# Four split tiles in place of two for the out-projection's activations, converted one weight slot ahead

## The chip, the cores and the metric

The kernel runs on one core of one Trainium2 chip. The metric is the device time of one execution in microseconds (us), taken as the median of several runs.

## What is computed

The reference is a two-layer backbone. Each layer has three parts, each a residual update of the token stream: a SwiGLU FFN, a mixer (a Fourier half and an mLSTM half with four heads), and a second FFN. 512 latent and 256 context tokens are 6 tiles of 128 rows, 1024 channels wide, all in float32. What matters here is the last step of every part, a product with an output weight, and the normalized, gated add behind it:

```python
def swiglu(h, w_in_ff, w_out_ff):
    gu = h @ w_in_ff
    g, u = gu[..., :D_FF], gu[..., D_FF:]
    return (jax.nn.silu(g) * u) @ w_out_ff          # D_FF = 2816

def _ffn_sublayer(x, mod, j, nw_pre, nw_post, w_in_ff, w_out_ff):
    shift, scale, gate = _mod(mod, j)
    y = swiglu(_pre(x, nw_pre, shift, scale), w_in_ff, w_out_ff)
    return x + FFN_RES * gate * rmsnorm(y, nw_post)
...
    return jnp.concatenate([yf, ym], axis=-1) @ w_out   # the mixer's last step
```

## The kernel before

**Split operands.** Every large product runs as three TensorE products of rounded operands: hi·hi, hi·lo and lo·hi, where hi is the operand copied to the engine's reduced float32 form and lo is what the copy lost. ScalarE (ACT) makes each hi with a copy, VectorE (DVE) each lo with a subtraction.

**Weight slots.** Weights come in slots of 128 x 2048 values (1 MB). There is one landing buffer `raw` and there are two pairs `w_hi`, `w_lo`. SyncE (SP) issues the load of slot n once `w_lo` of slot n - 1 is done (L981 for the out-projection). ACT makes `w_hi` (L1021) when the load has landed and TensorE has used slot n - 2. DVE makes `w_lo` behind it (L1183). Only the end of `w_lo` frees `raw`, so loading, `w_hi` and `w_lo` of successive slots follow each other in a ring.

**The out-projection.** A part has two token groups (g = 0, 1) of three tiles each; the last part has one group of four tiles, and the mixer of layer 1 has three tiles and then one. A group runs through `k_slots` weight slots: 11 in an FFN, 4 in a mixer. A slot has two halves (c = 0, 1), each one 128-row chunk of the contraction. `project_out` (L1428) waits for the slot's `w_lo`, then for each half waits for that half's `hj_lo`, and issues 18 matmuls of 128x512 (3 tiles, 3 products, 2 output halves). It raises the semaphore `w_used` after each half.

**The split activations.** `hj` (ACT L1023, DVE L1186) splits one 128x384 chunk of the hidden activations into `hj_hi[b]` and `hj_lo[b]`, b = 0 or 1. Half hs uses tile hs mod 2, and its conversion waits until half hs - 2 has been used:

```python
act.wait_ge(S["w_used"], hs - 1 + START)
```

The engines' queues are in order. In a slot s both ACT and DVE do: `hj` of the slot's own second half, then the weight split of slot n + 1, then `hj` of the next slot's first half. In the mixer's first group the first two are done earlier (`first_out`).

**What else stands in these queues.** In the first group of the first slots DVE reads two gate rows (`gate_half`, L1231) that TensorE has made after the slot. In both FFNs of layer 0 the first eight slots of the first group also hold a *modulation unit* each (L1197 and L1209, fed by loads of `w_ada`); after every fourth, TensorE sums its result (`finish_col`, L1452) before it goes on. Between the groups `evacuate` copies the three output tiles out of PSUM on DVE (L1293), and ACT takes their mean squares (L1067). In the second group the first slots carry *stages* of the first group's normalization behind their conversions: the gated product on DVE (L1268), the residual add on GpSimd (L1006), statistics on ACT (L1051), and transposes on TensorE (L1481).

Of the kernel before, what the change touches and what calls it, by code (L numbers as in the profile page):

```python
# [28 lines left out]
P = 128  # L29
# [9 lines left out]
GW = 384  # L39
# [121 lines left out]
def build(nc, x_in, w_ada, norm_w, w_ff_in, w_ff_out, w_in, w_gates, w_out, w_qkv, cvec_in, gate_b_in,  # L161
          b_col_in, nw_col_in, convw_in, convb_in, hn_w_in, fmix_in, dft_l_in, dft_c_in, dft_g_in, tri_in, out):
    ctx = ExitStack()
    with ctx:  # L164
# [7 lines left out]
        xn_lo = inner.enter_context(nc.sbuf_tensor("xn_lo", [P, KC, TOK], F32R))  # L172
        inner.close()
        arena = sb("arena", [P, XN + 2 * HG])
        hj_hi = [sb(f"hj_hi{i}", [P, GW], F32R) for i in range(2)]
        hj_lo = [sb(f"hj_lo{i}", [P, GW], F32R) for i in range(2)]
        raw = sb("raw", [P, SLOT])
        w_hi = [sb(f"w_hi{i}", [P, SLOT], F32R) for i in range(2)]
        w_lo = [sb(f"w_lo{i}", [P, SLOT], F32R) for i in range(2)]
# [830 lines left out]
        def _(act):  # L1010
# [12 lines left out]
            def hj(sub, g, c, hs, b):  # L1023
                if g == 0:

                    if sub["kind"] == "ffn":
                        act.wait_ge(S["h_done"], c + (sub["proj"] + 1))
                    elif c < HEADS:
                        act.wait_ge(S["f_sb"], HEADS * sub["mix"] + c + 1)
                    else:  # L1030
                        act.wait_ge(S["mix_done"], HEADS * sub["mix"] + c - HEADS + 1)

                act.wait_ge(S["w_used"], hs - 1 + START)
                w = sub["groups"][g] * P
                nc.scalar.activation(split_h(sub, b)[0][:, 0:w], hidden(sub, g, c), ACT.Copy).then_inc(S["hj_hi"], 1)  # L1035

# [62 lines left out]
            def first_out(sub):  # L1099

                nb = sub["slot"] + sub["in_slots"]
                for c in range(2):
                    hj(sub, 0, c, 2 * nb + c, c)

            for t in range(NT):
                act.dma_start(x[:, t, :], x_in[t]).then_inc(S["x_in"], 16)
# [14 lines left out]
            for sub in SUBS:  # L1121
# [18 lines left out]
                for g in range(len(sub["groups"])):  # L1140
                    nb = n0 + sub["in_slots"] + g * sub["k_slots"]
                    pb = nb % 2
                    early = sub["kind"] == "mix" and g == 0
                    if not early:
                        hj(sub, g, 0, 2 * nb, 0)
                    if g == 1:
                        evacuate(sub, 0)
                    done = 0
                    for s, n, par, half, u, st in out_steps(sub, g, loop, 0):
                        if not (early and s == 0):  # L1150
                            hj(sub, g, s * 2 + 1, n * 2 + 1, 1)
                        split_w(n + 1, (pb + par + 1) % 2)
                        if not (isinstance(s, int) and s == sub["k_slots"] - 1):
                            hj(sub, g, s * 2 + 2, n * 2 + 2, 0)
                        if st is not None:
                            stage(sub, 0, st)
                            done = st + 1
# [13 lines left out]
        def _(dve):  # L1171
# [14 lines left out]
            def hj(sub, g, c, q, hs, b):  # L1186
                w = sub["groups"][g] * P
                hi, lo = split_h(sub, b)
                dve.wait_ge(S["hj_hi"], q + 1)
                dve.wait_ge(S["w_used"], hs - 1 + START)  # L1190
                nc.vector.tensor_tensor(lo[:, 0:w], hidden(sub, g, c), hi[:, 0:w].bitcast(F32), ALU.subtract).then_inc(S["hj_lo"], 1)  # L1191

            def unit(count, u):
# [103 lines left out]
            def first_out(sub):  # L1297

                nb = sub["slot"] + sub["in_slots"]
                for c in range(2):  # L1300
                    hj(sub, 0, c, sub["hj"] + c, 2 * nb + c, c)


            dve.wait_ge(S["consts"], 16 * 8)
# [23 lines left out]
            for sub in SUBS:  # L1328
# [29 lines left out]
                for g in range(len(sub["groups"])):  # L1358
                    nb = n0 + sub["in_slots"] + g * sub["k_slots"]
                    q0 = sub["hj"] + g * 2 * sub["k_slots"]  # L1360
                    pb = nb % 2
                    early = sub["kind"] == "mix" and g == 0
                    if not early:
                        hj(sub, g, 0, q0, 2 * nb, 0)
                    if g == 1:
                        evacuate(sub, 0)
                    done = 0
                    for s, n, par, half, u, st in out_steps(sub, g, own.loop, 0):
                        if not (early and s == 0):
                            hj(sub, g, s * 2 + 1, s * 2 + (q0 + 1), n * 2 + 1, 1)  # L1370
                        split_w(n + 1, (pb + par + 1) % 2)
                        if not (isinstance(s, int) and s == sub["k_slots"] - 1):
                            hj(sub, g, s * 2 + 2, s * 2 + (q0 + 2), n * 2 + 2, 0)
                        if not sub["final"] and g == 0 and isinstance(s, int) and s < 2:
                            gate_half(sub, s, 6)
                        if half is not None:
                            unit(4 * half[2] - 16 + u, u)
                            if u == 3:
                                finish_col(half[2], half[1], 6)
                        if st is not None:  # L1380
                            stage(sub, 0, st)
                            done = st + 1
# [15 lines left out]
        def _(pe):  # L1398
# [28 lines left out]

            def project_out(sub, g, s, n, par, q0, first, last):  # L1428

                halves = [split_h(sub, c) for c in range(2)]  # L1430
                hi = w_hi[par][:].rearrange("p (c n) -> p c n", c=2)
                lo = w_lo[par][:].rearrange("p (c n) -> p c n", c=2)
                pe.wait_ge(S["w_lo"], n + 1 + START)
# [204 lines left out]
```

## Time and profile before

| What | Value |
|---|---|
| Median of 3 runs | 3081.69 us (3077.54 to 3083.17) |
| Span of the profiled execution | 3078.4 us |
| TensorE busy | 2796.1 us (91%) |
| DVE busy | 1455.6 us (47%) |
| ACT busy | 839.5 us (27%) |
| GpSimd busy | 84.6 us (3%) |
| Mean granted TensorE clock | 0.958 of full |

The span is from the first to the last instruction of one execution; it is the only time of that execution in the profile. Matmuls overlap in the trace, so a busy TensorE may still be short of its pace; the waits and the start times tell more than the busy share. The eleven stretches in which `project_out` runs take 101 to 111 us per FFN group of three tiles, 36 to 42 us per mixer group, and 121 us for the last part.

### The profile page before, as it was taken

What the parts mean: (1) busy time and instruction counts of PE and PEld (TensorE: products, weight loads), DVE (VectorE), ACT (ScalarE), POOL (GpSimd) and SP (SyncE); (2) the same over time, 40 slices, a digit from 0 to 9 for tenths busy, and PEclk for the clock granted to TensorE, in tenths of its full rate; (3) what the DMA queues carried; (4) which work ended last, traced back from release to release, by engine and by line L of the source; (5) the groups of instructions that cost most, each with busy time, mean ns of one, the idle gap of its engine ahead of it and who ended that gap; (6) DMA issues with size and microseconds to landing.
All of it is one profiled execution on the core that took longest, in us unless ns stands there. A gap on an engine that the chain in (4) does not pass through costs nothing. (4 is left out here: it accounts for less than half of the span.)

```text
span 3078.4 us, 35860 instructions
## 1 busy us (share of the span) xinstructions
PE 2796.1 (91%) x14352; PEld 2474.5 (80%) x14352; DVE 1455.6 (47%) x1975; ACT 839.5 (27%) x1128; POOL 84.6 (3%) x40
## 2 busy tenths in 40 slices
PE   5999999898988869999999899999997978599997
PEld 2999997777865769999877799998777756388876
DVE  2454546455444455455554545542355555532232
ACT  3211112443322431111224311112343522422222
POOL 0000000000000010000000100000001000100001
PEclk9999999998988989999999999999998999799999
DMA  5233344332200213333332233422332300222222
GB/s 208 83 117 129 109 136 127 106 110 73 76 1 1 96 69 115 131 109 132 120 131 96 96 123 109 136 84 81 109 105 91 103 1 28 82 97 98 100 87 82
DMA packets 98664, 298.95 MB, mean 97 GB/s; under 512 B 6672, under 2 KB 23056, under 8 KB 87056
## 3 DMA queue, kind: packets, MB, share of 16 engines
q1 hardware_dynamic: 91440, 280.42, 26.7%
q10 hardware_dynamic: 7136, 17.30, 1.6%
q8 instruction: 62, 1.02, 0.1%
q14 instruction: 26, 0.21, 0.0%
HBM read 295.60 MB, written 2.10 MB: 97 GB/s over the span
## 5 line engine op out<-in xcount | busy, mean ns | idle before, releaser
L1423 PE MATMUL ps<-xn_hi,w_hi 128*128 128x384 f32 (+2 forms) x2496 | 705.9, 345 | 33.2 <-DVE xn_lo L1261 19.6
L1423 PE MATMUL ps<-xn_lo,w_hi 128*128 128x384 f32 (+2 forms) x2496 | 701.6, 343 | 0.0
L1423 PE MATMUL ps<-xn_hi,w_lo 128*128 128x384 f32 (+2 forms) x2496 | 701.4, 343 | 0.0
L1183 DVE TENSOR_TENSOR w_lo<-raw,w_hi 128x2048 fp32r<-128x2048 f32 x195 | 444.8, 2281 | 358.9 <-ACT w_hi L1021 356.1
L1423 PEld LDWEIGHTS ps<-xn_hi,w_hi 128*128 128x128 f32 x2496 | 459.1, 190 | 48.0 <-DVE xn_lo L1261 20.8
L1423 PEld LDWEIGHTS ps<-xn_lo,w_hi 128*128 128x128 f32 x2496 | 460.0, 190 | 12.3
L1423 PEld LDWEIGHTS ps<-xn_hi,w_lo 128*128 128x128 f32 x2496 | 459.7, 190 | 12.5
L1021 ACT ACTIVATE w_hi<-raw 128x2048 fp32r<-128x2048 f32 x195 | 369.7, 1896 | 216.2 <-DMA raw<-w_ff_out 87.5
L1442 PE MATMUL ps<-w_hi,hj_hi 128*128 128x512 f32 x952 | 312.4, 410 | 78.6 <-DVE hj_lo L1191 65.8
L1209 DVE SCALAR_TENSOR_TENSOR acc<-raw_ada,silu_c,acc 128x512 f32<-128x512 f32 x512 | 345.5, 746 | 4.6 <-DVE acc L1197 3.2
L1442 PE MATMUL ps<-w_lo,hj_hi 128*128 128x512 f32 x952 | 303.8, 401 | 0.0
L1442 PE MATMUL ps<-w_hi,hj_lo 128*128 128x512 f32 x952 | 303.0, 400 | 0.0
L1136 ACT ACTIVATE arena<-ps 128x384 f32 (+1 forms) x132 | 57.6, 489 | 883.0 <-PE ps L1423 883.0
L1442 PEld LDWEIGHTS ps<-w_hi,hj_hi 128*128 128x128 f32 x952 | 177.8, 194 | 136.2 <-DVE hj_lo L1191 64.7
L1442 PEld LDWEIGHTS ps<-w_lo,hj_hi 128*128 128x128 f32 x952 | 185.2, 195 | 41.0
L1442 PEld LDWEIGHTS ps<-w_hi,hj_lo 128*128 128x128 f32 x952 | 184.9, 194 | 40.8
L1352 DVE TENSOR_TENSOR arena<-arena,ps 128x384 f32 (+1 forms) x132 | 67.3, 551 | 286.9 <-ACT arena L1136 284.9
L1006 POOL TENSOR_TENSOR x<-x,arena 128x1024 f32<-128x1024 f32 x32 | 83.9, 2625 | 2989.9 <-DVE arena L1268 2989.9
L1191 DVE TENSOR_TENSOR hj_lo<-arena,hj_hi 128x384 fp32r<-128x384 f32 (+1 forms) x164 | 87.9, 541 | 151.6 <-ACT hj_hi L1035 135.2
L1035 ACT ACTIVATE hj_hi<-arena 128x384 fp32r<-128x384 f32 (+2 forms) x164 | 82.3, 505 | 214.4 <-PE ps L1442 214.3
L760 PE MATMUL ps<-xn_hi,w_hi 128*128 128x384 f32 (+1 forms) x320 | 105.0, 368 | 13.3 <-DVE xn_lo L1261 9.8
L1222 DVE TENSOR_TENSOR vecs<-ps,b_col 128x8 f32 (+1 forms) x36 | 6.0, 166 | 209.5 <-PE ps L1452 208.0
(190 smaller groups left out, 2388.3 us busy)
## 6 DMA issues: line engine op xcount, KB each, us to landing
raw<-w_ff_in SPq DMA_DIRECT2D x88, 1024.0 KB, 5.4
raw<-w_ff_out SPq DMA_DIRECT2D x77, 1024.0 KB, 4.9
raw_ada<-w_ada SPq DMA_DIRECT2D x128, 512.0 KB, 3.8
raw<-w_out SPq DMA_DIRECT2D x16, 1024.0 KB, 4.8
raw<-w_in SPq DMA_DIRECT2D x12, 1024.0 KB, 5.3
arena<-w_ada SPq DMA_DIRECT2D x4, 2048.0 KB, 17.4
gate_row<-norm_w ACTq DMA_DIRECT2D x12, 512.0 KB, 4.3
arena<-dft_l_in ACTq DMA_DIRECT2D x2, 2048.0 KB, 8.1
```

The source lines that it names most:

```text
L760: ins = mm(ps[:, ch % 3 + 3 * g, 0:wd], w[:, k, c * P:(c + 1) * P], xx[:, k, g * GW:g * GW + wd], start=(k == 0 and i == 0), stop=(k == KC ...
L1006: nc.gpsimd.tensor_tensor(x[:, t, :], x[:, t, :], ys(i), ALU.add).then_inc(S["x_new"], 1)
L1021: nc.scalar.activation(w_hi[par][:, 0:width], raw[:, 0:width], ACT.Copy).then_inc(S["w_hi"], 1)
L1035: nc.scalar.activation(split_h(sub, b)[0][:, 0:w], hidden(sub, g, c), ACT.Copy).then_inc(S["hj_hi"], 1)
L1136: ins = nc.scalar.activation(dst, ps[:, s * 4 + 2 * g, 0:w], ACT.Silu)
L1183: nc.vector.tensor_tensor(w_lo[par][:, 0:width], raw[:, 0:width], w_hi[par][:, 0:width].bitcast(F32), ALU.subtract).then_inc(S["w_lo"], 1)
L1191: nc.vector.tensor_tensor(lo[:, 0:w], hidden(sub, g, c), hi[:, 0:w].bitcast(F32), ALU.subtract).then_inc(S["hj_lo"], 1)
L1209: ins = nc.vector.scalar_tensor_tensor(out=acc[:, s, :], in0=raw_ada[u % 2][:, c, :], scalar=silu_c[:, k, s:s + 1], in1=acc[:, s, :], op0= ...
L1222: nc.vector.tensor_tensor(dst, ps[:, bank_, GW:GW + 8].rearrange("p (c s) -> p c s", s=2), bias, ALU.add).then_inc(S["fin_read"], 1)
L1352: ins = nc.vector.tensor_tensor(hd, hd, ps[:, s * 4 + 2 * g + 1, 0:w], ALU.mult)
L1423: ins = mm(ps[:, 4 * b + 2 * g + c, col:col + wd], w[:, k, c, :], xx[:, k, t0:t0 + wd], start=(k == 0 and i == 0), stop=(k == KC - 1 and i ...
L1442: ins = mm(ps[:, 2 * i + hf, :], xx[:, i * P:(i + 1) * P], w[:, c, hf * 512:(hf + 1) * 512], start=first and c == 0 and a == 0, stop=last ...
```

## The change

`hj_hi` and `hj_lo` get four tiles each. Slot parity `par` uses tiles 2·par and 2·par + 1, so a conversion waits for half hs - 4 to have been used. Both conversions of a slot are moved into the slot before it: the first half's ahead of that slot's weight split, the second half's behind it. A group's first two conversions both stand at its start, ahead of `evacuate`. In the last part the tiles are slices of `xn_hi` and `xn_lo`, as before, now four of them. The scratch that the compiler keeps for dynamic DMA is set to 4096 bytes.

```diff
-        hj_hi = [sb(f"hj_hi{i}", [P, GW], F32R) for i in range(2)]
-        hj_lo = [sb(f"hj_lo{i}", [P, GW], F32R) for i in range(2)]
+        hj_hi = [sb(f"hj_hi{i}", [P, GW], F32R) for i in range(4)]
+        hj_lo = [sb(f"hj_lo{i}", [P, GW], F32R) for i in range(4)]
...
-                act.wait_ge(S["w_used"], hs - 1 + START)
+                act.wait_ge(S["w_used"], hs - 3 + START)
...
                     if not early:
-                        hj(sub, g, 0, 2 * nb, 0)
+                        for c in range(2):
+                            hj(sub, g, c, 2 * nb + c, 2 * pb + c)
                     if g == 1:
                         evacuate(sub, 0)
                     done = 0
                     for s, n, par, half, u, st in out_steps(sub, g, loop, 0):
-                        if not (early and s == 0):
-                            hj(sub, g, s * 2 + 1, n * 2 + 1, 1)
-                        split_w(n + 1, (pb + par + 1) % 2)
-                        if not (isinstance(s, int) and s == sub["k_slots"] - 1):
-                            hj(sub, g, s * 2 + 2, n * 2 + 2, 0)
+                        more = not (isinstance(s, int) and s == sub["k_slots"] - 1)
+                        ahead = (pb + par + 1) % 2
+                        if more:
+                            hj(sub, g, s * 2 + 2, n * 2 + 2, 2 * ahead)
+                        split_w(n + 1, ahead)
+                        if more:
+                            hj(sub, g, s * 2 + 3, n * 2 + 3, 2 * ahead + 1)
...
-                halves = [split_h(sub, c) for c in range(2)]
+                halves = [split_h(sub, 2 * par + c) for c in range(2)]
...
-    nc = bacc.Bacc("TRN2", target_bir_lowering=False, num_devices=1)
+    nc = bacc.Bacc("TRN2", target_bir_lowering=False, num_devices=1, dynamic_dma_scratch_size=4096)
```

DVE's queue is changed in the same way as ACT's, which is shown.

## Rows read from the trace of the kernel before

**Rows 1.** The page's head.
```profile
span 3078.4 us, 35860 instructions
```

**Rows 2.** Waits of the whole run: us in total, times, longest us.
```profile
PE ps L1442 <- DVE hj_lo L1191: 65.8, 48, 4.1
```

**Rows 3.** Timeline, layer 1, first FFN, first group: start, length, instruction [idle <-releaser].
```profile
2213.93 2.29 DVE L1183 TENSOR_TENSOR w_lo<-raw,w_hi 128x2048 fp32r<-128x2048 f32 x1 [6.18 <-ACT w_hi L1021]
...
2216.83 0.70 PE L1442 MATMUL ps<-w_hi,hj_hi 128*128 128x512 f32 x2 [1.01 <-DVE hj_lo L1191]
...
2221.06 1.92 ACT L1021 ACTIVATE w_hi<-raw 128x2048 fp32r<-128x2048 f32 x1 [4.62 <-DMA raw<-w_ff_out]
...
2223.01 2.29 DVE L1183 TENSOR_TENSOR w_lo<-raw,w_hi 128x2048 fp32r<-128x2048 f32 x1 [5.86 <-ACT w_hi L1021]
2225.22 0.55 DVE L1191 TENSOR_TENSOR hj_lo<-arena,hj_hi 128x384 fp32r<-128x384 f32 x1
2225.69 1.22 DVE L1293 COPY arena<-ps 128x1024 f32<-128x1024 f32 x1
```

**Rows 4.** Timeline, layer 0, mixer, second group: one slot of its stage loop.
```profile
1046.93 2.29 DVE L1183 TENSOR_TENSOR w_lo<-raw,w_hi 128x2048 fp32r<-128x2048 f32 x1 [1.19 <-ACT w_hi L1021]
...
1049.80 1.28 DVE L1268 SCALAR_TENSOR_TENSOR arena<-arena,stat,gate_row 128x1024 f32<-128x1024 f32 x1
1051.16 2.39 POOL L1006 TENSOR_TENSOR x<-x,arena 128x1024 f32<-128x1024 f32 x1 [349.81 <-DVE arena L1268]
...
1055.39 1.90 ACT L1021 ACTIVATE w_hi<-raw 128x2048 fp32r<-128x2048 f32 x1
...
1056.13 0.73 PE L1442 MATMUL ps<-w_hi,hj_hi 128*128 128x512 f32 x2 [1.83 <-DVE hj_lo L1191]
```

**Rows 5.** Timeline, layer 0, first FFN, first group: stretch with modulation units.
```profile
481.92 2.74 DVE L1209 SCALAR_TENSOR_TENSOR acc<-raw_ada,silu_c,acc 128x512 f32<-128x512 f32 x4
...
485.18 0.73 PE L1442 MATMUL ps<-w_hi,hj_hi 128*128 128x512 f32 x2 [1.58 <-DVE hj_lo L1191]
...
492.22 1.92 ACT L1021 ACTIVATE w_hi<-raw 128x2048 fp32r<-128x2048 f32 x1 [2.05 <-DMA raw<-w_ff_out]
...
495.70 2.28 DVE L1183 TENSOR_TENSOR w_lo<-raw,w_hi 128x2048 fp32r<-128x2048 f32 x1
...
510.64 1.92 PE L1452 MATMUL ps<-ones,acc 128*128 128x1 f32 x16 [2.28 <-DVE acc L1209]
...
522.58 0.53 ACT L1035 ACTIVATE hj_hi<-arena 128x384 fp32r<-128x384 f32 x1 [3.57 <-PE ps L1442]
523.01 1.90 ACT L1021 ACTIVATE w_hi<-raw 128x2048 fp32r<-128x2048 f32 x1
```

**Rows 6.** Timeline, the copies between that FFN's two groups.
```profile
576.92 3.49 DVE L1293 COPY arena<-ps 128x1024 f32<-128x1024 f32 x3 [1.85 <-PE ps L1442]
```

**Rows 7.** Timeline, mixers: layer 0 first slot, weights, copies, last slot; layer 1 copies.
```profile
1009.08 2.29 DVE L1183 TENSOR_TENSOR w_lo<-raw,w_hi 128x2048 fp32r<-128x2048 f32 x1
...
1016.23 1.92 ACT L1021 ACTIVATE w_hi<-raw 128x2048 fp32r<-128x2048 f32 x1 [8.56 <-DMA raw<-w_out]
...
1039.22 3.48 DVE L1293 COPY arena<-ps 128x1024 f32<-128x1024 f32 x3
...
1076.29 1.90 ACT L1021 ACTIVATE w_hi<-raw 128x2048 fp32r<-128x2048 f32 x1
...
2626.39 0.28 DVE L1191 TENSOR_TENSOR hj_lo<-arena,hj_hi 128x128 fp32r<-128x128 f32 x1
2626.59 2.35 DVE L1293 COPY arena<-ps 128x1024 f32<-128x1024 f32 x2
```

**Rows 8.** Timeline, TensorE after a wait, second group of layer 0's first FFN.
```profile
584.79 1.21 PE L1442 MATMUL ps<-w_hi,hj_hi 128*128 128x512 f32 x2 [2.17 <-DVE hj_lo L1191]
...
586.66 1.05 PE L1442 MATMUL ps<-w_hi,hj_lo 128*128 128x512 f32 x2
...
588.32 0.62 PE L1442 MATMUL ps<-w_lo,hj_hi 128*128 128x512 f32 x2
```

More of the change, by code:

```diff
@@ L1102, in first_out @@
                 for c in range(2):
-                    hj(sub, 0, c, 2 * nb + c, c)
+                    hj(sub, 0, c, 2 * nb + c, nb % 2 * 2 + c)
             for t in range(NT):
@@ L1189, in hj @@
                 dve.wait_ge(S["hj_hi"], q + 1)
-                dve.wait_ge(S["w_used"], hs - 1 + START)
+                dve.wait_ge(S["w_used"], hs - 3 + START)
                 nc.vector.tensor_tensor(lo[:, 0:w], hidden(sub, g, c), hi[:, 0:w].bitcast(F32), ALU.subtract).then_inc(S["hj_lo"], 1)
@@ L1300, in first_out @@
                 for c in range(2):
-                    hj(sub, 0, c, sub["hj"] + c, 2 * nb + c, c)
+                    hj(sub, 0, c, sub["hj"] + c, 2 * nb + c, nb % 2 * 2 + c)
             dve.wait_ge(S["consts"], 16 * 8)
@@ L1363, in _ @@
                     if not early:
-                        hj(sub, g, 0, q0, 2 * nb, 0)
+                        for c in range(2):
+                            hj(sub, g, c, q0 + c, 2 * nb + c, 2 * pb + c)
                     if g == 1:
@@ L1368, in _ @@
                     for s, n, par, half, u, st in out_steps(sub, g, own.loop, 0):
[L1369 to L1373, printed above, removed]
+                        more = not (isinstance(s, int) and s == sub["k_slots"] - 1)
+                        ahead = (pb + par + 1) % 2
+                        if more:
+                            hj(sub, g, s * 2 + 2, s * 2 + (q0 + 2), n * 2 + 2, 2 * ahead)
+                        split_w(n + 1, ahead)
+                        if more:
+                            hj(sub, g, s * 2 + 3, s * 2 + (q0 + 3), n * 2 + 3, 2 * ahead + 1)
                         if not sub["final"] and g == 0 and isinstance(s, int) and s < 2:
```

## The prediction

> **What bounds the kernel now.** I read the list of waits first. Its largest entry for TensorE in the out-projection says that `project_out` waited 65.8 us for `hj_lo`, in 48 places [rows 2]. The change aims at just that wait, so the question is what stood behind it. A wait is charged to whatever came last, and `hj_lo` of the next slot's first half is queued on DVE right behind `w_lo` of that slot.
>
> The timeline of a plain stretch answers it [rows 3]. `w_lo` starts at 2213.93 and ends at 2216.22; TensorE starts the slot at 2216.83, released by the `hj_lo` behind it. Then ACT sits idle until the next load lands at 2221.06, 4.8 us after the `w_lo` that freed `raw`; `w_hi` takes 1.9 us; the next `w_lo` starts at 2223.01. One turn of this ring (load, hi, lo) is 2223.01 - 2213.93 = 9.1 us, and nothing of it waits for TensorE. TensorE needs less: the ACT row at 522.58 shows 3.57 us idle after a 0.53 us conversion, both released by halves, so one half is 4.1 us and a slot 8.2 us [rows 5]. TensorE therefore waits about 0.9 us in each such slot whatever the order of the conversions. With `hj_lo` out of the way, it will be `w_lo` that it waits for.
>
> In a slot with a stage the ring is longer [rows 4]: `w_lo` at 1046.93, the gated product at 1049.80, GpSimd's add from 1051.16 to 1053.55, statistics, then `w_hi` at 1055.39 and the next `w_lo` at 1057.32. That is 10.4 us, with no TensorE in it either.
>
> So a gain can only come where TensorE is in the chain, and a loss wherever a conversion is put ahead of something in the chain of DVE and ACT.
>
> **The change part by part.**
>
> *Ring-bound slots.* ACT and DVE still do two conversions per slot. On ACT the two stand between one `w_hi` and the next, in the 4.8 us of the load (2 x 0.4 us) [rows 3]; in a stage slot one stands ahead of `w_hi`, as now [rows 4]. The pace stays 9.1 and 10.4 us. TensorE begins each slot some 0.5 us sooner and idles as much longer. At the end of an FFN's second group this is not even worth 0.5 us, because DVE still makes the next `w_lo` before its copies. Cost and gain: 0. If the cover were gone (a load under 0.9 us), each slot would pay up to 0.9 us.
>
> *Both FFNs of layer 0, first group.* Here TensorE is in the chain. In slot 1 it waits 1.58 us for a second-half `hj_lo` that stands behind a modulation unit ending at 481.92 + 2.74 = 484.66 [rows 5]. In the new order that conversion is ahead of the unit, so the gate row that TensorE makes after the slot, and the next unit behind it on DVE, come 1.7 us sooner (the idle plus the lost overlap between matmuls). Then `w_lo` of slot 3, now at 495.70, is held by `w_hi`, which the load lets start at 492.22: it can start at 492.22 + 1.92 + 0.03 = 494.17, a gain of 1.5 us. Ring, unit 3 and the summing at 510.64, which TensorE awaits, shift by that 1.5 us. At 522.58 ACT waits for TensorE to free a weight pair, converts, and only then makes `w_hi` at 523.01. The conversion moves ahead of that wait: 0.43 us more [rows 5]. The ring carries it to unit 7, whose sum TensorE awaits too. After that TensorE alone sets the pace to the group's end, and the copies wait for it with DVE idle 1.85 us, so there is room for the one conversion that now stands ahead of them (0.47 us) [rows 6]. The second group follows the copies. Gain: 1.53 + 0.43 = 1.96 us, twice, 3.9 us in all. I read the same order of rows in both FFNs.
>
> *Layer 1, first FFN.* No units, so the first slots are held by the gate rows, whose time does not move, and the rest by the ring. The copies at 2225.69 come 0.47 us after the start of the `hj_lo` at 2225.22, directly behind `w_lo` [rows 3]. The new order puts a second conversion there: loss 0.47 us, and the whole second group, started by the copies, comes that much later.
>
> *Mixer, layer 0.* DVE is busy up to 1009.08, where `w_lo` of slot 1 starts; now `hj_lo` goes first: +0.47 us. The next `w_hi` waits 8.56 us for its load [rows 7], so the ring takes the delay over and passes it through two more turns to the `w_lo` ahead of the copies at 1039.22, where a second conversion adds another 0.47 us. In the last slot, `w_hi` at 1076.29 runs straight behind a conversion [rows 7]; this slot no longer has one: -0.42 us (the step from hi conversion to `w_hi`, the same as 522.58 to 523.01 [rows 5]). Net +0.52 us.
>
> *Mixer, layer 1.* The same, with 128x128 conversions in the second group: one takes 2626.59 - 2626.39 = 0.20 us [rows 7]. +0.47 + 0.20 - 0.20 = +0.47 us.
>
> *Last part.* Its halves have four tiles, so 4.1 x 4/3 = 5.5 us each and 10.9 us a slot: longer than the ring's 9.1 us. TensorE sets the pace and no conversion is late. 0. *Scratch:* no DMA is issued by GpSimd in this kernel, and the added tiles only move addresses. 0; what this could cost has no row, and I take none.
>
> **The sum.** -3.92 + 0.47 + 0.52 + 0.47 = -2.46 us on the span of 3078.4 us [rows 1], so 3075.9 us. The median of the runs is 3.3 us above that span; the same distance gives 3081.7 - 2.5 = 3079.2 us.
>
> **TensorE's clock.** After an idle time of 2.17 us its pairs of matmuls stand at the lower level, 1.2 GHz: lengths of 1.05 us until 588.32, where they are 0.62 us again, at 2.4 GHz [rows 8]. By a half of 4.1 us a pair takes 0.46 us at the high level; two low ones between 586.66 and 588.32 take 0.83 us each. Four of them lose 1.6 us. After 1.83 us idle there is no such stretch [rows 4]. This opens both ends of the ring-free terms. In the layer 0 FFNs TensorE's second wait for a sum gets shorter (about 0.4 us), and the low stretch behind it may vanish: down to -1.6 us each. The first gets longer, by 0.8 us, since TensorE comes to it sooner: up to +0.8 us of low pace each (two pairs). I take 0 for both, as those waits exist already.
>
> In a stage slot the change joins two short waits into one of 10.4 - 8.2 = 2.2 us, which is past the 2.17 us of [rows 8]. A low stretch of 1.6 us fits in those 2.2 us, so I count nothing. The Trainium skill (TensorE: Matmul & The Clock Gate, HAM oscillation) says that a loop which waits for data in every turn starts each turn at the low clock, and pays the transition every time. By this rule each stage slot would pay; the trace agrees for single waits [rows 8], but not for a whole loop.
>
> **Rivals.**
>
> *A. The wait for `hj_lo` is real time.* For it: 65.8 us, the largest wait in the out-projection [rows 2]. Against: the 9.1 us ring in [rows 3] has no TensorE and no conversion in it. If all of it came back, 3081.7 - 65.8 = 3015.9 us. Chance 0.10.
>
> *B. The joined waits hold the clock low through whole slots (slower).* At 0.83 us a pair a slot of 18 pairs takes 14.9 us, 4.5 us past the stage slot's 10.4 us. It decides from 2.2 us of lost pace per slot, 6 low pairs. Three stage slots in each of four groups lose 13.5 us per group; the FFNs win back 0.9 us in each of 7 later slots: 3 x 7.2 + 13.5 = 35 us, 3117 us. Against: the low stretches in the trace end after a few us of matmuls [rows 8]. Chance 0.06, with slower turns of unknown cause in it. The page's rule above would act here.
>
> *C. Layer 0's gain does not come.* If something else holds unit 3 (its own load, or a low clock over the whole first sum), only the delays are left: +1.5 us, 3083.2 us. Chance 0.12.
>
> *D. The clock helps.* The low stretches behind the second sums vanish: -2.5 - 3.2 = -5.7 us, 3076.0 us, at the edge of what can be told. Chance 0.08.
>
> **Chances and range.** My forecast has 0.64. 0.2% is 6.2 us, about what a measurement of this kernel can tell from no change (the three runs spread over 5.6 us). Faster by more: A and half of D, 0.14. Slower: B, 0.06. Within 0.2%: 0.80. Around the forecast the clock bounds give -2.5 - 3.2 and -2.5 + 1.6, and C +1.5; with half the spread of the runs (2.8 us) on each side, -8.5 to +4.3 us at most. I take 3073 to 3084 us, with A and B left out.
>
> **What would show it.** Right: the entry of `hj_lo` for L1442 nearly gone, and waits for `w_lo` L1183 of 40 us or more in its place; starts of `w_lo` still 9.1 to 9.5 us apart in plain stretches and 10.4 in stage slots; the copies of layer 0's FFNs 2 us sooner after their group's start, those of layer 1's FFN and the mixers 0.5 to 0.9 us later. Wrong: `w_lo` starts closer together (A), pairs of 1.05 us length through whole stage slots (B), the sum at 510.64 not moved against the group's start (C), or loads that take longer than 4.8 us.

## The result and the profile after

| | Before | After |
|---|---|---|
| Median of 18 runs each | 3079.53 us (3075.39 to 3085.27) | 3085.23 us (3082.29 to 3087.62) |
| Ratio after/before, 95% interval | | 1.0019 (1.0012 to 1.0026) |
| Span of the profiled execution | 3078.4 us | 3082.6 us |
| Mean granted TensorE clock | 0.958 | 0.957 |

The change makes the kernel 5.7 us slower, where I forecast 2.5 us faster. That is inside the 0.2% that I called hard to tell, but the interval excludes no change, and 3085 us lies above my range. My kernel before, by its first three runs, stood at 3081.7 us; 18 runs put it at 3079.5 us.

The page's head and the waits of the whole run (us in total, times, longest us), after:

```profile
span 3082.6 us, 35860 instructions
...
ACT w_hi L1021 <- DMA raw<-w_ff_out: 214.2, 42, 8.0
...
PE ps L1448 <- DVE w_lo L1186: 53.4, 37, 4.6
...
PE ps L1448 <- DVE hj_lo L1194: 7.9, 3, 3.1
```

The `hj_lo` entry of [rows 2] (65.8 us, 48 times) has shrunk to 7.9 us in 3 waits; `w_lo` stands in its place with 53.4 us. The wait changed its name, as forecast. ACT's wait for the load was 87.5 us before. It grew mainly because the second half's conversion, which used to break this idle time in two, now stands ahead of it.

Timeline, layer 1, first FFN, first group, which answers to [rows 3]:

```profile
2205.38 2.29 DVE L1186 TENSOR_TENSOR w_lo<-raw,w_hi 128x2048 fp32r<-128x2048 f32 x1 [6.32 <-ACT w_hi L1021]
...
2207.82 0.72 PE L1448 MATMUL ps<-w_hi,hj_hi 128*128 128x512 f32 x2 [1.08 <-DVE w_lo L1186]
...
2214.72 2.29 DVE L1186 TENSOR_TENSOR w_lo<-raw,w_hi 128x2048 fp32r<-128x2048 f32 x1 [6.11 <-ACT w_hi L1021]
...
2223.91 2.29 DVE L1186 TENSOR_TENSOR w_lo<-raw,w_hi 128x2048 fp32r<-128x2048 f32 x1 [6.43 <-ACT w_hi L1021]
...
2226.12 1.02 DVE L1194 TENSOR_TENSOR hj_lo<-arena,hj_hi 128x384 fp32r<-128x384 f32 x2
2227.05 3.48 DVE L1296 COPY arena<-ps 128x1024 f32<-128x1024 f32 x3
```

The pace of `w_lo` is 9.2 to 9.3 us in these rows and up to 9.6 us in this group's other ring-bound slots; before it was 9.1 to 9.7 us. From the last `w_lo` to the copies it is 2227.05 - 2223.91 = 3.14 us, against 2225.69 - 2223.01 = 2.68 us in [rows 3]: the second conversion ahead of the copies costs 0.46 us.

Timeline, layer 0, first FFN, first group, which answers to [rows 5]:

```profile
502.49 0.61 PE L1448 MATMUL ps<-w_hi,hj_lo 128*128 128x512 f32 x2
506.13 2.66 PE L1458 MATMUL ps<-ones,acc 128*128 128x1 f32 x16 [3.03 <-DVE acc L1212]
508.65 1.20 PE L1448 MATMUL ps<-w_hi,hj_hi 128*128 128x512 f32 x2
```

TensorE waits 3.03 us for the first sum where it waited 2.28 us, and the sum's sixteen narrow matmuls take 2.66 us where they took 1.92 us [rows 5]. The granted clock in the sum was 0.68 here and 1.00 before.

**Where the time is lost.** The last load of the same FFN's second group (slot 43) shows it. After, then before, timeline:

```profile
660.24 2.29 DVE L1186 TENSOR_TENSOR w_lo<-raw,w_hi 128x2048 fp32r<-128x2048 f32 x1 [1.25 <-ACT w_hi L1021]
...
662.56 0.37 SPq L981 DMA_DIRECT2D raw<-w_ff_out  x1
...
668.88 1.92 ACT L1021 ACTIVATE w_hi<-raw 128x2048 fp32r<-128x2048 f32 x1 [7.86 <-DMA raw<-w_ff_out]
```
```profile
663.87 2.29 DVE L1183 TENSOR_TENSOR w_lo<-raw,w_hi 128x2048 fp32r<-128x2048 f32 x1 [1.50 <-ACT w_hi L1021]
...
671.20 1.92 ACT L1021 ACTIVATE w_hi<-raw 128x2048 fp32r<-128x2048 f32 x1 [3.80 <-DMA raw<-w_ff_out]
```

From the end of `w_lo` to the start of `w_hi` it is 668.88 - 662.53 = 6.35 us after and 671.20 - 666.16 = 5.04 us before. I call this span the load's time from here on. The DMA view of the same stretch (660 to 674 us; the GB/s digits are 40 slices of 0.35 us), after and then before:

```profile
GB/s 0 0 0 0 0 0 0 0 0 0 187 35 164 316 386 374 445 410 410 211 35 23 23 23 0 0 0 0 0 0 0 0 0 0 0 0 0 0 0 0
...
q8 instruction: 1, 0.02, 0.8%
...
raw<-w_ff_out SPq DMA_DIRECT2D x1, 1024.0 KB, 6.3
```
```profile
GB/s 445 386 304 82 12 0 0 0 0 0 0 0 0 0 0 0 0 0 0 0 82 12 176 328 398 421 433 410 410 328 47 0 0 0 0 0 0 0 0 0
...
q8 instruction: 1, 0.02, 0.4%
...
raw<-w_ff_out SPq DMA_DIRECT2D x1, 1024.0 KB, 5.0
```

Both stretches hold one packet of queue q8, 16 KB of kind "instruction". It is a block of TensorE's own code: the experiments below that add instructions to TensorE's queue alone move it. After, the load runs at 400 GB/s and then drags on at 23 to 35 GB/s for four slices, about what one of the sixteen engines moved while the load ran (430 / 16 = 27 GB/s); before, it ends at once. Narrower windows place the block. After it falls in the load's first 2 us (662.5 to 664.5), before only in 670 to 672, when the load that began at 666.16 is all but done. After and before:

```profile
q8 instruction: 1, 0.02, 5.4%
```
```profile
q8 instruction: 1, 0.02, 3.0%
```

The first share is larger because the block itself took 1.74 us there, against 0.96 us before. Among the out-projection's slots this repeats: the loads of slots 43, 99, 102, 143, 146 and 158 take 6.35, 5.45, 6.19, 5.99, 6.25 and 6.31 us. Together that is 6.4 us over six loads of 5.03 us. (Slot 55's took 5.66 us, with its block moved 4.2 us behind the load's start; it was not late when the kernel ran again.)

A late load can cost more than its own delay. Behind slot 43's, TensorE waited 2.15 us, and then four pairs of matmuls ran at 1.2 GHz, so that the copies between the groups waited for it:

```profile
673.18 0.74 PE L1448 MATMUL ps<-w_hi,hj_hi 128*128 128x512 f32 x2 [2.15 <-DVE w_lo L1186]
...
674.95 1.05 PE L1448 MATMUL ps<-w_hi,hj_hi 128*128 128x512 f32 x2
```

How I read the earlier move: TensorE's code stream had been held, once a slot, at the wait for the second half's `hj_lo`. In the kernel before, the blocks in these loads are moved 4.2 to 4.7 us behind a load's start, which is when the first half ends. After the change nothing holds the stream inside a slot; it is held at the wait for `w_lo` and let go when the next load begins. By the matmuls begun when a given block is moved, the blocks of the second groups and of slot 158 are moved 11 to 29 matmuls sooner (for instance after 3213 in place of 3225, and after 2963 in place of 2989). In the FFNs' first groups they shift by three at most, for a reason that I did not find.

### The profile page after: what moved, and what is told of

The parts are those of the page before. It is cut to its first block and busy times, and to the rows that moved or that the text cites. A ratio compares the mean times of both kernels' runs of the same rounds, so it can differ in the third digit from the quotient of the medians.

```text
span 3082.6 us, 35860 instructions
## 1 busy us (share of the span) xinstructions
PE 2792.0 (91%) x14352; PEld 2474.4 (80%) x14352; DVE 1451.8 (47%) x1975; ACT 833.8 (27%) x1128; POOL 84.6 (3%) x40
## 5 line engine op out<-in xcount | busy, mean ns | idle before, releaser
L1448 PE MATMUL ps<-w_hi,hj_hi 128*128 128x512 f32 x952 | 311.3, 409 | 78.6 <-DVE w_lo L1186 53.4
L760 PE MATMUL ps<-xn_lo,w_hi 128*128 128x384 f32 (+1 forms) x320 | 100.6, 355 | 0.0
```

Of the source, the lines that this page charges most:

```text
L760: ins = mm(ps[:, ch % 3 + 3 * g, 0:wd], w[:, k, c * P:(c + 1) * P], xx[:, k, g * GW:g * GW + wd], start=(k == 0 and i == 0), stop=(k == KC ...
L1448: ins = mm(ps[:, 2 * i + hf, :], xx[:, i * P:(i + 1) * P], w[:, c, hf * 512:(hf + 1) * 512], start=first and c == 0 and a == 0, stop=last ...
```

## The experiments

Times from here on are ratios to the kernel before on the same chip. The late loads are those of one profiled execution each. A load is listed as late if it took over 5.6 us. Two kinds are left out: stage slots, where ACT makes `w_hi` only after 6.2 us in any case, and slot 152, a load of the mixer's input weights that is late in eight of the twelve kernels with one landing buffer, the kernel before among them (it comes back at the end).

### Parts of the change

**The changed kernel again.** Measured: 3087.55 us, ratio 1.0024 (1.0012 to 1.0037).

> The changed kernel once more, to see what repeats from execution to execution. Theory 1 (TensorE's instruction blocks): the loads of the last slots of the second FFN groups that took 6.0 to 6.35 us in the first trace instead of 5.0 (slots 43, 102, 143, 146 and 158 of all weight slots) are late again, each with a 16 KB instruction block moved in the first 2 us of the load; time +5 to +6 us against before. Rival 2 (chance): other slots are late, or none, and the difference to before is nearer to my sum of -2.5 us.

The loss repeats. Its late loads are those of slots 43, 99, 102, 143, 146 and 158: the same six.

**Layout alone.** Four tiles by slot parity and the smaller scratch, but the waits and the order of before:

```diff
+def ahead_group(sub, g):
+    return False
...
+                back = 3 if ahead_group(sub, g) else 1
...
-                act.wait_ge(S["w_used"], hs - 3 + START)
+                act.wait_ge(S["w_used"], hs - back + START)
```

> Four tiles and the small DMA scratch, but the waits and the order of the kernel before everywhere. Theory 1: 0 +- 1 us against before, and no load over 5.6 us in the out-projections. Rival 3 (the layout itself costs: other addresses, less scratch): +5 us or more, as the whole change.

Measured: 3077.41 us, ratio 0.9997 (0.9985 to 1.0008). Tiles and scratch cost nothing that can be told. Not every load stayed under 5.6 us, as I had expected: slot 54's took 5.82 us, with no block in it, and slot 96's, in a stage slot, 6.42 us.

**The two halves of the new order.** First the new order only in the first groups of layer 0's FFNs, then only everywhere else:

```diff
-    return False
+    return bool(sub["ada_out"]) and g == 0
```

The complement:

```diff
-    return bool(sub["ada_out"]) and g == 0
+    return not (sub["ada_out"] and g == 0)
```

> The new order and the four-deep wait only in the first groups of layer 0's two FFNs, where the modulation units stand; everything else in the order of before. My sum says -3.9 us, and theory 1 adds nothing, since the second groups read their instructions as before: -3 to -4 us against before. Rival 3 (layout): above 0. If my gain was overrated: between -2 and 0.

> The complement: the order of before in the two groups with modulation units, the new one everywhere else. My sum alone says +1.5 us. Theory 1 adds some five to seven late loads of 1.0 to 1.3 us: +7 to +9 us. Rival 4 (the loss sits in the modulation groups and the second groups are innocent): +1 to +2 us.

Measured: 3077.15 us, ratio 0.9998 (0.9989 to 1.0007), against 3086.63 us, ratio 1.0024 (1.0014 to 1.0034). The first has no late load, the second the same six as the changed kernel. The loss is wholly in the second part (both ran beside the same kernel before); the gain of 3.9 us that I forecast for the first does not show: it is 0.6 us less, within -3.4 to +2.2.

### Moving TensorE's block edges

If the block's timing is the cause, instructions that do nothing must change which loads are late. They stand at the head of TensorE's queue, where it waits for its first data anyway:

```diff
             pe.sem_inc(S["w_used"], START)
+            for _i in range(24):
+                pe.sem_inc(S["pad"], 1)
```

> The changed kernel with 24 more instructions at the head of TensorE's queue, where it waits for its first data until 18 us in any case; nothing else differs. Theory (some weight loads are late because TensorE's next instruction block is moved in their first 2 us): all later block edges stand 24 instructions, about a third of a slot of 74 or some 3 us, earlier. The late loads of slots 43, 99, 102, 143, 146 and 158 fall from 6.0 to 6.3 us to at most 5.3 us. Blocks that were moved 4.2 to 4.5 us behind a load's start (slots 30, 33, 89, 92, 136) may come into the first 2 us and make those loads late; in slots with modulation units that costs nothing, at slot 136 up to 1.5 us. Time: 2 to 6 us less than the changed kernel, 3079 to 3083.5 us. Rival (the order of the conversions itself makes the loads or the copies late): the same six slots are late and the time is that of the changed kernel, 3084 to 3087 us.

> As the run before, with 48 instructions, about two thirds of a slot or some 6 us. Theory: the blocks of slots 43, 99, 102, 143, 146 and 158 are now moved 3 to 5 us behind the start of the preceding slot's load, and none that was seen elsewhere comes into a load's first 2 us, so that at most one or two loads are late by a microsecond: 3 to 7 us less than the changed kernel, 3078 to 3082.5 us. Rival: 3084 to 3087 us, with the same six late loads.

> The kernel before with the same 24 instructions. Theory: a block's move there is tied to the end of the wait for the second half's activations, 4.1 to 4.8 us behind the load's start, or falls outside the loads; the shift changes which slots have it. Where it now falls behind the wait for the weights it can hit a load's first 2 us too, in up to three slots: within 0 to 3 us of the kernel before, either side at most 0.1 percent. Rival (the extra instructions cost or give something by themselves): the same difference of several us as between the two shifted versions of the changed kernel and the changed kernel itself.

| Version | Ratio (95%) | Late loads, slots |
|---|---|---|
| changed, + 24 | 1.0023 (1.0014 to 1.0032) | 33, 45, 55, 89, 136, 146 (and 3) |
| changed, + 48 | 1.0012 (1.0003 to 1.0021) | 39, 42, 98 (and 3) |
| before, + 24 | 1.0008 (0.9999 to 1.0017) | none |

Where the late loads are is mostly as forecast: 43, 99, 102, 143 and 158 are repaired by 24 instructions, and 33, 89 and 136 take their place. But 146 stayed late, and 45 and 55 came unforeseen. With 48, none of the six is late, but three others are, where I expected one or two. The times missed. With 24 I expected 2 to 6 us less than the changed kernel, and it is the same; with 48 the ratio fell by 0.0007, some 2 us, where I expected 3 to 7 us. One cause is that I had counted late loads in the groups with modulation units at nothing. With slot 89 late, the first group of layer 0's second FFN took 112.0 us here and 111.6 us in a version below, against 108.8 to 109.6 us in the four kernels with the new order there and neither a late load, added matmuls nor added waits. Slot 33's cost is not settled: its group took 110.1 us, and the same in a version below without it. Slot 33's load, after and then with 24 instructions more:

```profile
559.45 2.29 DVE L1186 TENSOR_TENSOR w_lo<-raw,w_hi 128x2048 fp32r<-128x2048 f32 x1 [4.92 <-ACT w_hi L1021]
566.75 1.92 ACT L1021 ACTIVATE w_hi<-raw 128x2048 fp32r<-128x2048 f32 x1 [6.93 <-DMA raw<-w_ff_out]
```
```profile
562.83 2.29 DVE L1186 TENSOR_TENSOR w_lo<-raw,w_hi 128x2048 fp32r<-128x2048 f32 x1 [4.91 <-ACT w_hi L1021]
571.45 1.92 ACT L1021 ACTIVATE w_hi<-raw 128x2048 fp32r<-128x2048 f32 x1 [8.24 <-DMA raw<-w_ff_out]
```

Here the changed kernel's load takes 566.75 - 561.74 = 5.01 us, and the padded one's 571.45 - 565.12 = 6.33 us. The two kernels differ in nothing but the 24 instructions, and so in where the block edges fall.

### Holding the code stream again

TensorE waits, ahead of a slot's second half, for its own first half. First in the second groups alone (`g == 1`), then in every group but the last part's:

```diff
                 for c in range(2):
+                    if c == 1 and g == 1:
+                        pe.wait_ge(S["w_used"], 2 * n + 1 + START)
                     pe.wait_ge(S["hj_lo"], s * 2 + (q0 + c + 1))
```

> The changed kernel in which TensorE, in the second groups, waits ahead of a slot's second half until its own first half is used. It adds no work of another engine; it holds TensorE's instruction stream where the old wait for the second half's activations held it. The order of the conversions, the tiles and the first groups are those of the changed kernel. Theory (with the old hold gone, the block of instructions is asked for right behind a slot's start and makes that slot's load late): in the second groups the blocks are moved 4 to 5 us behind a load's start again, the loads of slots 43, 99, 102, 143, 146 and 158 take 4.9 to 5.2 us, and the time falls by 5 to 8 us to 3077 to 3081 us, a wait more for TensorE notwithstanding. Rival (the conversions' new order costs the time by itself, or the block's place in the code does and not when it is asked for): the six loads stay late and the time is 3084 to 3088 us.

> The changed kernel with the hold ahead of the second half in every group but the last part's, the first groups too. With the hold in the second groups alone, their late loads went and the three second groups took 6.9 us less together, but the added instructions shifted later block edges, and the loads of slots 55, 89 and 136 in the first groups, which were not held, became 1.1 to 1.7 us late. Theory (a block asked for behind the weights' wait makes that load late, and the hold moves it behind the first half wherever it stands): no load outside slots 3 and 152 takes over 5.5 us, and the whole now shows what the groups showed, 3 to 8 us under the changed kernel: 3077 to 3082 us, ratio to the kernel before 0.9985 to 1.0005. Rival (the order costs its 6 us in the whole, whatever the loads do): ratio 1.0010 to 1.0025 again.

| Version | Ratio (95%) | Late loads, slots |
|---|---|---|
| held in second groups | 1.0010 (1.0001 to 1.0019) | 55, 89, 136 |
| held in all groups | 1.0007 (0.9998 to 1.0016) | none |

Held in the second groups, their late loads go, and the three FFN second groups together take 7.0 us less than in the changed kernel's first profile and 3.8 us less than in its second. The load of slot 43, which answers to that above, takes 671.23 - 666.19 = 5.04 us:

```profile
663.90 2.29 DVE L1186 TENSOR_TENSOR w_lo<-raw,w_hi 128x2048 fp32r<-128x2048 f32 x1 [1.33 <-ACT w_hi L1021]
...
671.23 1.92 ACT L1021 ACTIVATE w_hi<-raw 128x2048 fp32r<-128x2048 f32 x1 [6.54 <-DMA raw<-w_ff_out]
```

But the added waits shift the edges too, so three first groups got late loads, and the ratio is 1.0010, some 3 us under the changed kernel's where I expected 5 to 8 us. Held everywhere, no load is late, and the ratio is 1.0007: most of the loss is back, and no change is inside the interval, but it is above my limit of 1.0005. The hold itself costs time in the first groups, and that can be read. The last pair of a slot's first half and the first of its second start 0.75 us apart with it, where pairs otherwise start 0.46 us apart; and the sums that follow it run slower (below). From the first out-projection matmul to the copies, the three FFN first groups took 110.1, 110.4 and 103.7 us, against 108.8, 109.0 and 102.2 us in the changed kernel.

Lengths of the three FFN second groups, from the start of the copies ahead of them to that of the copies behind, in us, with the late loads in them:

```
                         layer 0, first   layer 0, second   layer 1, first
before                   107.9            107.0             107.7
layout alone             106.6            107.3             106.5
new order, first groups  106.8            106.9             106.3
before + 24              107.9            107.4             107.4
changed                  109.5 (43)       109.9 (99, 102)   109.7 (143, 146)
changed again            107.8 (43)       110.1 (99, 102)   108.0 (143, 146)
new order, the rest      108.8 (43)       110.3 (99, 102)   109.5 (143, 146)
changed + 24             107.7            107.3             108.2 (146)
changed + 48             110.3 (39, 42)   108.3 (98)        106.9
held, second groups      108.0            106.6             107.5
held, all groups         107.5            106.8             107.8
filling matmuls (below)  109.9 (39, 42)   106.5             106.7
```

The 23 groups with no late load take 106.3 to 108.0 us, 107.2 on average; the 13 with one or two late loads take 107.8 to 110.3 us, 109.3 on average. The order of the conversions makes no difference to this: the eleven groups with the new order and no late load take 106.5 to 108.0 us as well.

### TensorE's clock at the modulation sums

Ten matmuls that nothing reads ahead of the first sum, five ahead of the second:

```diff
                             pe.wait_ge(S["fin_read"], half[2])
+                            for _i in range(10 if u == 3 and s == 3 else 10 // 2):
+                                mm(ps[:, 7, 0:P], ident[:], ident[:], start=True, stop=True)
                             finish_col(half[2], 4 * half[2] - 12, 6)
```

> The changed kernel with ten 128x128 matmuls of the identity, whose result nothing reads, ahead of TensorE's wait for the first modulation sum of each such group and five ahead of the second. By the 0.24 us of each in the gate rows they fill 2.4 of the 3.0 us wait and 1.2 of the 1.5 us. Theory (the modulation groups gained 1.0 in place of 1.96 us because the longer wait lets TensorE's clock fall before the sum): the first sum takes 1.9 in place of 2.7 us and the stretch at the low clock behind it is shorter by up to six pairs at 0.4 us, so that each of the two groups gains 0.7 to 3 us: 1.5 to 6 us less than the changed kernel's 3085, 3079 to 3083.5 us. Rival (the clock falls for the sum's own sixteen narrow matmuls, whatever stands ahead of them): the sum at 1.9 us or not, the low stretch stays, and the time is within 1.5 us of the changed kernel's.

Measured: 3080.62 us, ratio 1.0006 (0.9997 to 1.0016), some 4 us under the changed kernel. Timeline with the filling matmuls, first sum of layer 0's first FFN:

```profile
506.47 2.39 PE L1578 MATMUL ps<-ident 128*128 128x128 f32 x20
509.87 1.95 PE L1458 MATMUL ps<-ones,acc 128*128 128x1 f32 x16 [1.00 <-DVE acc L1212]
511.68 0.70 PE L1448 MATMUL ps<-w_hi,hj_hi 128*128 128x512 f32 x2
512.22 0.63 PE L1448 MATMUL ps<-w_lo,hj_hi 128*128 128x512 f32 x2
```

The sum takes 1.95 us in place of 2.66, and the pair behind it 0.63 us, the length at 2.4 GHz, with no low stretch at all. From the first sum to the second it is 36.6 us, against 39.4 us in the changed kernel and 38.1 us before. So the clock's fall costs the changed kernel 2.8 us in this group, 1.3 us more than it cost before; in the second FFN's group the stretch is 37.7 us against 39.7 us. The second sums, with five matmuls, were not helped: they took 2.1 and 2.7 us, with a low stretch behind each. The total is not clean, since this version's block edges moved as well (slots 39, 42, 88, 129, 151, 153 and 165 are late).

### Taking the load out of the ring

Two landing buffers by slot parity in the kernel before, in the changed kernel, and there with the filling matmuls:

```diff
-                    sp.wait_ge(S["w_lo"], n + START)
-                sp.dma_start(raw[:, 0:width], src).then_inc(S["w_raw"], 16)
+                    sp.wait_ge(S["w_lo"], n - 1 + START)
+                sp.dma_start(raw[par][:, 0:width], src).then_inc(S[f"w_raw{par}"], 16)
```

> The kernel before with two landing buffers in place of one, by slot parity (scratch 4096 to make room): the load of slot n waits for the split of slot n - 2, not n - 1. Nothing else differs. Theory (in the out-projection's plain and stage slots the ring of load 4.8, hi part 1.9 and lo part 2.3 us is the bound, 9.2 to 10.4 us a slot, and the waits for the second half's activations are slack in it): the load leaves the ring, slots go to TensorE's pace of 8.2 to 8.8 us, and the time falls by 0.5 to 1.2 us in each of some 60 to 75 slots: 35 to 75 us less, 3005 to 3045 us; the second half's waits now stand on the path where DVE or ACT come late. Rival (those waits bound the kernel, not the ring): under 10 us less, 3068 to 3080 us.

> The changed kernel with two landing buffers (scratch 2048 to make room). With two buffers the kernel before took 3045.2 us, and its trace shows TensorE waiting for the second half's activations on the path: 1.8 to 2.2 us in each stage slot and 0.8 to 1.1 us in every other plain slot. Theory (the change takes those waits away, and gave nothing with one buffer because the ring was the bound): some 17 stage slots by 1 to 2 us and some 20 plain slots by 0.3 to 0.8 us, less the copies that are 0.5 us later and a clock that falls a little more: 15 to 35 us less than 3045, so 3010 to 3030 us. Rival (something else sets the slots' pace, such as the clock or DVE's own work in the stages): within 5 us of 3045.

> Both: the changed order, two landing buffers and the filling matmuls. Theory: the parts add up, 1.5 to 6 us less than the changed kernel with two landing buffers. Rival: the same as that kernel within 1.5 us.

| Version | Median | Ratio (95%) |
|---|---|---|
| before, two buffers | 3045.23 us | 0.9889 (0.9874 to 0.9904) |
| changed, two buffers | 3037.50 us | 0.9865 (0.9850 to 0.9881) |
| and filling matmuls | 3036.64 us | 0.9863 (0.9847 to 0.9879) |

The last is the version that beats both: 42 us less than the kernel before. The ring was the bound: without it the kernel before gained 34.5 us, just under the 35 us that I had put as the least. With the ring gone the change is worth 0.24%, some 7.4 us. That is half of the least I expected. Stage slots explain it, as the timeline of the changed kernel with two buffers shows:

```profile
581.06 1.28 DVE L1273 SCALAR_TENSOR_TENSOR arena<-arena,stat,gate_row 128x1024 f32<-128x1024 f32 x1
582.50 2.39 POOL L1008 TENSOR_TENSOR x<-x,arena 128x1024 f32<-128x1024 f32 x1 [580.96 <-DVE arena L1273]
...
586.72 1.90 ACT L1023 ACTIVATE w_hi<-raw 128x2048 fp32r<-128x2048 f32 x1
...
588.66 2.29 DVE L1188 TENSOR_TENSOR w_lo<-raw,w_hi 128x2048 fp32r<-128x2048 f32 x1 [1.25 <-ACT w_hi L1023]
...
591.00 0.73 PE L1450 MATMUL ps<-w_hi,hj_hi 128*128 128x512 f32 x2 [2.01 <-DVE w_lo L1188]
```

`w_hi` is queued on ACT behind the statistics, which wait for GpSimd's add, which waits for the gated product, which DVE does behind `w_lo`. The slot stays 10.45 us long with one buffer or two, and the wait for `hj_lo` became one of 2.01 us for `w_lo`. Most of the gain is in the slots behind the stages. Each of the three second FFN groups takes 101.9 to 102.0 us in place of 103.5 to 103.6 us. Layer 1's first group, which has no stages, takes 95.3 us with either order, since with two buffers alone its slots already follow each other at 8.16 us. Behind the stages `w_lo` now comes at TensorE's own pace,

```profile
648.75 2.29 DVE L1188 TENSOR_TENSOR w_lo<-raw,w_hi 128x2048 fp32r<-128x2048 f32 x1 [1.10 <-ACT w_hi L1023]
...
654.97 1.92 ACT L1023 ACTIVATE w_hi<-raw 128x2048 fp32r<-128x2048 f32 x1 [3.61 <-PE ps L1450]
...
656.91 2.29 DVE L1188 TENSOR_TENSOR w_lo<-raw,w_hi 128x2048 fp32r<-128x2048 f32 x1 [4.93 <-ACT w_hi L1023]
```

656.91 - 648.75 = 8.16 us, with `w_hi` released by TensorE and not by a load. The filling matmuls add nothing that can be told here (-0.9 us, well inside the intervals), so the theory that the parts add up falls.

## Why the prediction was wrong

**What bounds the kernel: right.** The ring of load, hi and lo set the pace at 9.1 to 9.7 us a slot whatever the order of the conversions, and the wait of 65.8 us only changed its name. Two landing buffers show the ring as the bound. Rival A is refuted.

**Ring-bound slots, "Cost and gain: 0": the step that failed.** I took the load's 4.8 us as a constant of the ring; in six slots the span from the end of `w_lo` to `w_hi` became 5.45 to 6.35 us in place of 5.03 us. I weighed only what ACT and DVE do in it, and asked of the vanishing wait only what TensorE's matmuls lose. I did not ask what else the wait had timed. It had set when TensorE's code blocks are moved, on the same DMA engines as the load, which is the one step of the ring that nothing covers. That cost 6.4 us by the six loads. My list did name "loads that take longer than 4.8 us" as a sign of error, but I gave it no rival and no price; "slower turns of unknown cause" had a part of B's 0.06. What shows this step as the one that failed: the loss is in the part of the change outside layer 0's first groups (ratio 1.0024 against 0.9998), the late loads move with TensorE's block edges, and where none is late the second groups are as long as before.

**Layer 0's FFNs, first group, -1.96 us each: half of it came.** The conversion ahead of the unit works: in the first FFN, from the first gate row to the first sum it is 31.3 us in place of 33.1, a gain of 1.8 us where I had 1.53. But from the first sum to the second it is 39.4 us in place of 38.1. The clock term was mis-sized. I took 0 and allowed +0.8 us; it measured +1.3 us, because the sum itself slowed by 0.74 us and the low stretch behind it got longer. This repeats: the first sum took 2.5 to 3.0 us in all six groups of the three profiles with the new order there, and 1.92 to 1.94 us in all eight with the old one. Three profiles with the new order there (the changed kernel twice, and the first groups alone) against four with the old one: the first groups are shorter by 1.1 and 0.7 us on average.

**Layer 1's FFN, +0.47 us: right** for the step itself, 0.46 us; in the length of the group it is lost, 101.8 us against 101.6 us on average. Of the mixers' +0.52 and +0.47 us only one piece was seen, the -0.20 us at the end of layer 1's: 57.8 us between the copies against 58.0 us. The rest was not shown.

**The sum again:** the two first groups as measured, -1.1 and -0.7, the six late loads as measured, +6.4, and the three delays as forecast, +1.5: +6.1 us. The runs show +5.7 us. That they agree within 0.4 us is partly luck, since the delays are hardly measured and single groups vary by 1 us.

**The range.** My own bounds, -8.5 to +4.3 us around 3081.7 us, end at 3086.0 us, and I wrote 3084 without a reason. The time of 3085.2 us would lie inside the wider figure, but only because my kernel before was 2.2 us too high: the change of +5.7 us is outside +4.3 us too. A smaller slip: four low pairs lose 1.5 us by the row's 0.83 and 0.46 us, not 1.6.

**The rivals.** C had the sign and a figure (3083.2 us) near the result, but not the cause: its +1.5 us is there at most, beside a gain that half came. B: the joined waits of the changed kernel's stage slots, in the FFNs' second groups, were 1.6 to 2.0 us and not 2.2 us. Only one of nine, of 2.01 us, was followed by a low stretch, of four to five pairs and not of whole slots, and the slots stayed at 10.4 us. So what the Trainium skill (TensorE: Matmul & The Clock Gate, HAM oscillation) describes did not come about in this loop. The page's loop waits longer for its data than it computes, while TensorE works over 8 us here for each such wait, so the page is not refuted either. D: the second sum's wait did shorten, from 1.77 to 1.49 us, but its low stretch stayed.

**What stays open.** How TensorE's sequencer decides when to ask for a block; why a block moved late in a load is mostly harmless and in slot 152 never; and the time with 24 instructions more. Its median is some 7 us above the kernel before, but its only profiled execution was the fastest of eleven (3080.3 us against a median of 3085.2 us), so the group lengths can't account for the median.

## What to carry to other kernels

A wait that is slack for the arithmetic can still time something else: before you remove one, list all that its engine issues or fetches behind it, its own code included, and see which transfer runs at that moment. Where a single-buffered load is a step of the bounding ring, a single packet of another queue can stand on the critical path, so a second landing buffer (41 us here with the change, 34 us without) comes ahead of any reordering. If the time moves by a few us with no cause in the data flow, shift one engine's code by a few instructions and see whether the same places stay slow.

## What the runs showed of the hardware

Over the twelve profiled kernels with one landing buffer, these are the loads whose landing released `w_hi`, by when TensorE's 16 KB code block was moved, counted from the load's start (loads of over 7.5 us are left out):

```
block moved                loads   load's median   over 5.4 us
0.9 to 2.9 us behind          35         6.20 us   35 (longest 6.77 us)
0.6 us behind                  3         5.04 us   none
3.8 us behind or later       104         4.97 us   5 (5.51 to 6.97 us)
  the same, slot 152           8         6.57 us   8 (6.42 to 6.94 us)
no block                     531         5.00 us   13 (longest 5.82 us)
  the same, slot 152           4         5.37 us   2 (5.53 and 5.58 us)
```

So one packet of 16 KB, a sixty-fourth of the load's bytes, goes with a longer load, by 1.2 us at the median, whenever it comes 0.9 to 2.9 us into it. Slot 152 shows that this is not the whole rule: its block came at 4.0 to 4.7 us, and it too was some 1.2 us longer with a block than without. The block itself is often slow as well in the first class, 0.9 to 2.0 us, where otherwise it mostly takes 0.9 to 1.1 us. The tail of 23 GB/s suggests that the one DMA engine which carries the block falls behind with its share, while the load is done only when all sixteen are; that reading is argued from the rates, not tested alone.

The Trainium skill (Runtime: NRT & Kernel Launch, Instruction fetch mechanics) says that crossing such a block costs a DMA step which is mostly hidden. For TensorE's own stream nothing speaks against it here: its matmuls in `project_out` show no wait without a releaser, before or after. The cost fell on another queue's transfer.

A second finding is that behind the longer wait, 3.0 us in place of 2.3 us, TensorE's clock was lower already within the sixteen narrow matmuls (2.66 us in place of 1.92 us), and filling 2.4 us of that wait with matmuls that nothing reads kept it at 2.4 GHz through sum and slot. The length of this wait alone does not decide it. With the hold in all groups, the same sum took 3.54 us behind a wait of 2.19 us, which is shorter than the 2.28 us before:

```profile
508.31 3.54 PE L1460 MATMUL ps<-ones,acc 128*128 128x1 f32 x16 [2.19 <-DVE acc L1212]
```
